# Hybrid decoder step: the dilated samples' window loads are requested in the paged stage's rings, and the next step's keys are turned ahead of the weights

## The reference, cut to what matters

```
DILATIONS = ((128, 1), (512, 4), (2048, 16))
def _dilated_sample(q, k_all, v_all, window, dil, n_buf):
    n_keys = window // dil
    idx = n_buf + jnp.arange(t)[:, None] - dil * jnp.arange(n_keys + 1)[None, :]
    kg, vg = k_all[:, idx], v_all[:, idx]
    sc = jnp.einsum('bqhd,bqjhd->bhqj', q, kg) / math.sqrt(HEAD_DIM)
    m = jnp.max(sc, axis=-1, keepdims=True)
    pw = jnp.exp(sc - m)
    l = jnp.sum(pw, axis=-1, keepdims=True)
    o = jnp.einsum('bhqj,bqjhd->bqhd', pw / l, vg)
    lse = (m + jnp.log(l))[..., 0]
```

## Time and profile before

| | us |
|---|---|
| time, median of 3 runs | 3216.09 (3215.17 to 3216.36) |
| profiled execution, its own time | 3219.56 |
| profiled execution, its span | 3218.0 |
| TensorE busy in the span | 2900.9 (90%) |
| VectorE busy | 1656.6 (51%) |
| ScalarE busy | 1463.8 (45%) |
| GpSimd busy | 632.9 (20%) |

### The profile page before, as it was taken

How to read it: one execution, slowest core, us unless ns; L and a number is a source line. 1 busy time by engine, 2 the same in 40 slices (tenths; PEclk the granted TensorE clock), 3 DMA queues, 4 the chain that set the end, 5 groups by cost and what they waited for, 6 DMA issues and landing times. The chain is left out here.

```text
span 3218.0 us, 46966 instructions
## 1 busy us (share of the span) xinstructions
PE 2900.9 (90%) x17542; PEld 2089.2 (65%) x17542; DVE 1656.6 (51%) x2702; ACT 1463.8 (45%) x2550; POOL 632.9 (20%) x908
## 2 busy tenths in 40 slices
PE   7999969999899999998999958888888873799998
PEld 5888848888555555555888845555555441588887
DVE  2000032222688888887666645555555434666663
ACT  3222131111577777776556525555555423333332
POOL 0000001111122222221033343443333200000000
PEclk9999989999899999998999979999999986899999
DMA  6656655554301010103223329999999886333321
GB/s 202 207 204 210 223 186 196 198 192 170 120 1 40 1 40 1 43 8 82 75 71 81 81 92 421 420 420 420 420 421 420 351 329 223 130 104 104 104 84 41
DMA packets 209508, 574.12 MB, mean 178 GB/s; under 512 B 39840, under 2 KB 108928, under 8 KB 173472
## 3 DMA queue, kind: packets, MB, share of 16 engines
q0 software_dynamic: 45568, 348.22, 27.5%
q1 hardware_dynamic: 163744, 223.27, 21.1%
HBM read 494.67 MB, written 143.73 MB: 198 GB/s over the span
## 5 line engine op out<-in xcount | busy, mean ns | idle before, releaser
L1512 DVE COPY sbs_kT<-sbs_ps_T 128x512 f32<-128x512 f32 x256 | 271.9, 1094 | 267.8 <-PE sbs_ps_T L1674 267.7
L465 PE MATMUL proj_ps_G<-proj_w_hi,proj_xT_hi 128*128 128x512 f32 x1024 | 399.8, 390 | 1.6 <-DVE proj_xT_lo L326 1.6
L469 PE MATMUL proj_ps_G<-proj_w_hi,proj_xT_lo 128*128 128x512 f32 x1024 | 398.6, 389 | 0.0
L467 PE MATMUL proj_ps_G<-proj_w_lo,proj_xT_hi 128*128 128x512 f32 x1024 | 398.5, 389 | 0.0
L404 ACT ACTIVATE proj_out<-proj_ps_G,proj_stat 128x512 f32<-128x512 f32 (+1 forms) x136 | 93.5, 689 | 581.2 <-PE proj_ps_G L469 574.2
L1674 PE MATMUL sbs_ps_T<-held,sbs_k_ring 128*128 128x128 f32 x2048 | 281.5, 293 | 41.5 <-ACT sbs_kT L1595 39.1
L1674 PEld LDWEIGHTS sbs_ps_T<-held,sbs_k_ring 128*128 128x128 f32 x2048 | 250.4, 153 | 84.4 <-ACT sbs_kT L1595 42.1
L674 POOL CAST sbp_sp_hi<-sbp_sp 128x512 fp32r<-128x512 f32 (+3 forms) x320 | 172.3, 553 | 505.3 <-DVE sbp_sp L716 495.2
L1595 ACT ACTIVATE sbs_kT<-sbs_ps_T 128x512 f32<-128x512 f32 x256 | 260.1, 1115 | 5.2 <-PE sbs_ps_T L1674 4.9
L716 DVE SCALAR_TENSOR_TENSOR sbp_sp<-sbp_Z,sbp_el 128x512 f32<-128x512 f32 (+3 forms) x320 | 180.0, 603 | 118.9 <-ACT sbp_el L794 118.5
L465 PEld LDWEIGHTS proj_ps_G<-proj_w_hi,proj_xT_hi 128*128 128x128 f32 x1024 | 192.2, 188 | 41.3 <-DVE proj_xT_lo L326 1.8
(11 more groups left out here) (289 smaller groups left out, 5803.6 us busy)
## 6 DMA issues: line engine op xcount, KB each, us to landing
out_k_win_s<-in_cache_k_win POOLq DMA_DIRECT2D x16, 2044.0 KB, 8.3
out_v_win_s<-in_cache_v_win POOLq DMA_DIRECT2D x16, 2044.0 KB, 8.3
proj_out<-in_w_in SPq DMA_DIRECT2D x32, 512.0 KB, 5.7
dls_k_in<-in_cache_k_win SPq DMA_DIRECT2D x16, 1024.0 KB, 10.9
dls_v_in<-in_cache_v_win SPq DMA_DIRECT2D x16, 1024.0 KB, 14.6
merge_o<-scratch_o_dil SPq DMA_DIRECT2D x48, 256.0 KB, 4.7
proj_x_in<-in_x_prompt SPq DMA_DIRECT2D x16, 512.0 KB, 4.3
scratch_xT_hi<-proj_xT_hi SPq DMA_DIRECT2D x16, 512.0 KB, 4.8
```

The source lines that it names most:

```text
L465: nc.tensor.matmul(ps_G[0:n, g, :], xT_hi[:, slot, k, 0:n], w_hi[:, k, cols], start=(k == 0), stop=False)
L467: nc.tensor.matmul(ps_G[0:n, g, :], xT_hi[:, slot, k, 0:n], w_lo[:, k, cols], start=False, stop=False)
L469: mm = nc.tensor.matmul(ps_G[0:n, g, :], xT_lo[:, slot, k, 0:n], w_hi[:, k, cols], start=False, stop=(k == KC - 1))
L1512: nc.vector.tensor_copy(by_lane(kT[:, j, :, :])[:, :, i, :], ps_T[:, x % TB, :].rearrange("p (a n) -> p a n", a=PAIRS)).then_inc(kT_odd, 1)
```

## The change

It has five parts.

- The rings `k_ring` and `v_ring` of the paged stage are allocated outside it and are used by the dilated samples too, in place of `k_in` and `v_in`. `kT` holds one chunk instead of two. The identity matrix and `own` are read from `held`, where the paged stage has them already.
- SP requests the new queries and keys of the dilated samples in the paged stage, behind the store of sample 6.
- Once the last page has landed (`v_loaded[7]` at its last count), SP requests the 8 chunks of keys and the 8 chunks of values of step 0, 16 MB, still in the paged stage. The store of the last sample's row comes behind these 16 loads in SP's list, and the wait for all stores behind that.
- In the dilated samples SP loads the mask, the counts and `pick16`, then the new values; for step 1 each key chunk is requested when the slot's tiles of step 0 have been turned, and the value chunks after `weigh(0)`.
- The keys of (1,0) are turned, copied and scored ahead of turning the weights of step 0, on TensorE, ACT and DVE.

One clearing of semaphores with its barrier moves from between the paged stage and the dilated samples to between these and `merge`.

```diff
+def window_new(held):
+    at = 8 * W - 2 * W - 248
+    return held[0:NS, at:at + 2 * W].rearrange("p (i c) -> p i c", c=W)
+
+def window_chunk(src, b, c):
+    rows = src[0].rearrange("b s h d -> b s (h d)")
+    if c == 0:
+        return rows[b, WIN - 512:WIN, :].rearrange("(n p) c -> p n c", p=P)
+    return rows[b].rearrange("(p r) c -> p r c", r=16)[:, 0:DEC_S, :]
...
@@ stick_breaking_sample, SyncE @@
-            for b in range(DEC_B):
+            def store(b):
                 sp.wait_ge(row_copied, b + 1)
                 sp.dma_start(t["o_sb_s"][b * DEC_S:(b + 1) * DEC_S, :], o_row[:, :]).then_inc(stored, 16)
+
+            for b in range(DEC_B - 1):
+                store(b)
+            w_new = window_new(held)
+            sp.dma_start(w_new[:, 0, :], t["q_dl_s"]).then_inc(win_new_loaded, 16)
+            sp.dma_start(w_new[:, 1, :], t["k_win_s"][0].rearrange("b s h d -> b s (h d)")[:, WIN - DEC_S:WIN, :]) \
+                .then_inc(win_new_loaded, 16)
+            sp.wait_ge(v_loaded[RING - 1], 16 * (NC * N // RING))
+            for x in range(RING):
+                sp.wait_ge(k_turned, GP * (NC * N - RING + x + 1))
+                sp.dma_start(k_ring[:, x, :, :], window_chunk(t["cache_k_win"], x % NC, x // NC)).then_inc(win_k_loaded[x], 16)
+            for x in range(RING):
+                if x % NC == 0:
+                    sp.wait_ge(av_done, N - 1 + x // NC)
+                sp.dma_start(v_ring[:, x, :, :], window_chunk(t["cache_v_win"], x % NC, x // NC)) \
+                    .then_inc(win_v_loaded[x // NC], 16)
+            store(DEC_B - 1)
             sp.wait_ge(stored, 16 * DEC_B)
...
@@ dilated_sample @@
-        ident = m.sb("ident", [P, P])
+        ident, own = (paged_constants(held)[n] for n in ("ident", "own"))
...
-        k_in = m.sb("k_in", [P, E, NA, W])
-        v_in = m.sb("v_in", [P, 2, E, NA, W])
-        v_new = m.sb("v_new", [DEC_S, E, W])
-        kT = m.sb("kT", [P, 2, E, PAIRS, 512])
+        kT = m.sb("kT", [P, E, PAIRS, 512])
...
@@ dilated_sample, SyncE @@
-            sp.dma_start(ident[:, :], t["ident"][:, :]).then_inc(new_loaded, 16)
-            sp.dma_start(qk_new[:, 0, :], t["q_dl_s"]).then_inc(new_loaded, 16)
-            sp.dma_start(qk_new[:, 1, :], k_new).then_inc(new_loaded, 16)
+            for buf, n in ((mask, "win_mask"), (count, "win_count"), (pick, "pick16")):
+                sp.dma_start(buf[:, :], t[n][:, :]).then_inc(consts, 16)
             for st in range(STEPS):
-                for c in range(2):
-                    for e in range(E):
-                        if st + c > 0:
-                            sp.wait_ge(turned, tile_of(st, c, e, 0) - (E - 1) * NA)
-                        sp.dma_start(k_in[:, e, :, :], chunk(k_c, E * st + e, c)).then_inc(k_loaded[e], 16)
-                    if st == 0 and c == 0:
-                        for buf, n in ((mask, "win_mask"), (count, "win_count"), (own, "own_head4"), (pick, "pick16")):
-                            sp.dma_start(buf[:, :], t[n][:, :]).then_inc(consts, 16)
                 if st > 0:
+                    for c in range(2):
+                        for e in range(E):
+                            sp.wait_ge(turned, tile_of(st - 1, c, e, NA - 1) + 1)
+                            sp.dma_start(k_ring[:, E * c + e, :, :], window_chunk(t["cache_k_win"], E * st + e, c)) \
+                                .then_inc(k_loaded[E * c + e], 16)
                     sp.wait_ge(av_done, st)
-                for c in range(2):
-                    for e in range(E):
-                        sp.dma_start(v_in[:, c, e, :, :], chunk(v_c, E * st + e, c)).then_inc(v_loaded[c], 16)
...
+                    for c in range(2):
+                        for e in range(E):
+                            sp.dma_start(v_ring[:, E * c + e, :, :], window_chunk(t["cache_v_win"], E * st + e, c)) \
+                                .then_inc(v_loaded[c], 16)
+                sp.dma_start(v_new[:, :, :], v_new_d[E * st:E * st + E].rearrange("b s c -> s b c")) \
+                    .then_inc(v_new_loaded, 16)
...
@@ dilated_sample, VectorE, in weights(st) behind the maximum @@
+                if st + 1 < STEPS:
+                    keys_to_sbuf(dve, nc.vector.tensor_copy, 1, st + 1, 0)
                 dve.wait_ge(exp_done, st + 1)
...
@@ dilated_sample, ScalarE @@
                 nc.scalar.activation(s[:, :], s[:, :], ACT.Exp, bias=stat[:, st, 0:1]).then_inc(exp_done, 1)
+                if st + 1 < STEPS:
+                    keys_to_sbuf(act, plain, 0, st + 1, 0)
...
@@ dilated_sample, TensorE @@
+            turn_keys(0, 0)
+            score(0, 0)
             for st in range(STEPS):
-                for c in range(2):
-                    turn_keys(st, c)
-                    score(st, c)
+                turn_keys(st, 1)
+                score(st, 1)
+                if st + 1 < STEPS:
+                    turn_keys(st + 1, 0)
+                    score(st + 1, 0)
                 turn_weights(st)
                 weigh(st)
...
@@ build @@
-            stick_breaking_sample(nc, t, held, paged_loaded)
-        nc.clear_and_free_semaphores([dil_qk_loaded, paged_loaded])
...
+            with nc.sbuf_tensor("sbs_k_ring", [P, 8, 4, W], F32) as k_ring, nc.sbuf_tensor("sbs_v_ring", [P, 8, 4, W], F32) as v_ring:
+                stick_breaking_sample(nc, t, held, paged_loaded, k_ring, v_ring, win_k_loaded, win_v_loaded, win_new_loaded)
+                dilated_sample(nc, t, held, k_ring, v_ring, win_k_loaded, win_v_loaded, win_new_loaded)
+        nc.clear_and_free_semaphores([dil_qk_loaded, paged_loaded, win_new_loaded] + win_k_loaded + win_v_loaded)
         nc.all_engine_barrier()
-        dilated_sample(nc, t)
         merge(nc, t)
```

More of the change, by code:

```diff
@@ L1328, in _, with stick_breaking_sample @@
                         turn_in(p + 1, f, OB[:, :])
-def stick_breaking_sample(nc, t, held, paged_loaded):
+def window_new(held):
[6 more added lines that the diff above has]
+    return rows[b].rearrange("(p r) c -> p r c", r=16)[:, 0:DEC_S, :]
+def stick_breaking_sample(nc, t, held, paged_loaded, k_ring, v_ring, win_k_loaded, win_v_loaded, win_new_loaded):
     C = H * DEC_S
@@ L1750, in _, with dilated_sample @@
             pick_rows(DEC_B - 1)
-def dilated_sample(nc, t):
+def dilated_sample(nc, t, held, k_ring, v_ring, k_loaded, v_loaded, new_loaded):
     C = H * DEC_S
@@ L1764, in dilated_sample @@
         m = Mem(nc, ctx, "dls")
-        ident = m.sb("ident", [P, P])
+        ident, own = (paged_constants(held)[n] for n in ("ident", "own"))
         mask = m.sb("mask", [P, KEYS])
         count = m.sb("count", [P, KEYS])
-        own = m.sb("own", [P, W])
         pick = m.sb("pick", [P, E * DEC_S])
-        qk_new = m.sb("qk_new", [NS, 2, W])
+        qk_new = window_new(held)
+        v_new = held[0:DEC_S, 2 * W - 384:6 * W - 384].rearrange("p (e c) -> p e c", c=W)
         q_pad = m.sb("q_pad", [P, DEC_B, PAIRS * (C + 8)])
@@ L1819, in dilated_sample @@
         TILES_PER_STEP = 2 * E * NA
[L1821 to L1827 removed]
+        v_new_d = t["v_win_s"][0].rearrange("b s h d -> b s (h d)")[:, WIN - DEC_S:WIN, :]
         block = ctx.enter_context(nc.Block())
@@ L1923, in plain @@
                 return nc.scalar.activation(out, src, ACT.Copy)
+            keys_to_sbuf(act, plain, 0, 0, 0)
             for st in range(STEPS):
-                for c in range(2):
-                    keys_to_sbuf(act, plain, 0, st, c)
+                keys_to_sbuf(act, plain, 0, st, 1)
                 act.wait_ge(max_done, st + 1)
                 nc.scalar.activation(s[:, :], s[:, :], ACT.Exp, bias=stat[:, st, 0:1]).then_inc(exp_done, 1)
+                if st + 1 < STEPS:
+                    keys_to_sbuf(act, plain, 0, st + 1, 0)
                 act.wait_ge(p_turned, st + 1)
@@ L1953, in turn_keys @@
                             pe.wait_ge(copied[(tt - 3) % 2], (tt - 3) // 2 + 1)
-                        if st > 0 and tt - TILES_PER_STEP * st < 3:
+                        if st > 0 and c == 1 and tt - tile_of(st, 1, 0, 0) < 3:
                             pe.wait_ge(p_copied[0], st)
@@ L1972, in score @@
                         mm = nc.tensor.matmul(Sc[e * C:(e + 1) * C, c, :], q_pad[:, E * st + e, pr * C:(pr + 1) * C],
-                                              kT[:, c, e, pr, :], start=(pr == 0), stop=(pr == PAIRS - 1))
+                                              kT[:, e, pr, :], start=(pr == 0), stop=(pr == PAIRS - 1))
                 if c == 1:
@@ L2004, in weigh @@
                         mm = nc.tensor.matmul(O[e * C:(e + 1) * C, :], pT[:, x, e * C:(e + 1) * C],
-                                              v_in[:, x // NA, e, x % NA, :], start=False, stop=(x == NT - 1))
+                                              v_ring[:, E * (x // NA) + e, x % NA, :], start=False, stop=(x == NT - 1))
                 mm.then_inc(av_done, 1)
@@ L2524, in build @@
             dilated_prompt(nc, t, held, dil_qk_loaded, paged_loaded)
```

(10 more changed lines are left out.)

33 lines of the change are left out of this document (10 added, 23 removed).

## The result

| | before | changed |
|---|---|---|
| median, us | 3215.17 (3207.44 to 3216.36, 5 runs) | 3232.51 (3229.27 to 3235.54, 5 runs) |
| profiled execution, its own time | 3219.56 | 3230.36 |
| its span | 3218.0 | 3228.5 |

The ratio is 1.0062, 95% interval 1.0049 to 1.0075: 15.8 to 24.1 us slower on 3215.17. The two medians are 17.3 us apart. The forecast was 3232.1, 16.0 us slower, from a median before of 3216.09.

A forecast was written before the change was run, and what follows sets the result against it. DMA bounds the paged stage's end, while the dilated samples are a chain with waits. A 29.3 us later start less 13.3 saved gives +16.0 on the median 3216.09: 3232.1 us, range 3222 to 3240.

The forecast's parts named there:

- The store behind the loads: End of paged stage: last store lands only with the 16 loads, so the dilated samples begin 29.3 us later.
- The rival that SP is only held in its issue: End of paged stage: store lands once SP's last load is accepted; +1.0 us in all, 3217.1; chance 0.05.
- Start of the stage: Dilated samples: first scores 12.0 us behind the start instead of 18.0, saving 6.0 us.
- Turn (0,1): Dilated samples: this turn of keys falls from 10.71 to 8.66 us, saving 2.05.
- The gap: Dilated samples: keys of (1,0) handled in the gap of the weights; 24.3 us become 22.4, saving 1.9.
- First weighing: Dilated samples, weigh(0): at full clock 8.2 us instead of 11.49, saving 3.3.
- Behind the weighing nothing changes: Dilated samples after weighing: no change in time; step 1's values just hidden, new values' row first on the queue.
- The sum: Whole kernel: 29.3 us later start less 13.3 us saved in the stage, +16.0 us.
- the rival on bandwidth: The 16 early loads run at 332 GB/s because chunks of 2 KB and 8 KB rows mix; +26, 3242 us; chance 0.04.

The follow-up runs named there:

- half the loads: Changed kernel with step 0's eight value loads moved to the dilated samples, last store on SP behind the eight key loads: ratio 0.9990, median 3211.49 us.
- another queue: Changed kernel with the last sample's store issued by ScalarE on its own queue: 1.0001; with only key loads in the paged stage as well: 0.9978.
- the late wait: Only key loads early, SP's loads reordered: last store moved from ScalarE to SP, its landing waited for at the dilated samples' end; 0.9937, median 3195.87 us.
- two runs: Changed kernel with the last store on ScalarE's queue (1.0001, median 3214.69 us), or on SP between key and value loads (1.0004, 3215.21 us).
- the two runs with the old order: Changed kernel with keys of (1,0) turned and scored behind weighing step 0 again: 1.0060, median 3235.32 us; on a slower chip 1.0035.
- the run with the new values first: Changed kernel with step 1's new values loaded ahead of its eight value loads: 1.0021 on a slower chip, beside 1.0034 for the changed kernel there.

## Why the prediction was right, step by step

- **The store behind the loads: right.** It was forecast to land with the last load, 44.8 us behind the first key load's issue; it was 44.2. The loads were to begin 14.1 us ahead of the copied row; 14.1. Behind the landing I had taken 1.9 us of barriers, with the clearing that moves; it was 1.16. So the start came 28.0 us later, not 29.3. The store landed 0.1 us behind the last load, and the experiments with half the loads, another queue and the late wait show that it is this wait. The forecast wanted the store issued after 2590; 2587.26 is 6.1 us early like everything in this trace.
- **The rival that SP is only held in its issue: wrong as the whole, right as a part.** SP's last load was accepted at 2587.21, 13.2 us behind the row. Had the store alone been mended, this limit would have stood in its place and taken all the gain, as two runs showed.
- **Start of the stage: saved 6.0 forecast, 6.3 measured** (scores 11.69 us behind the first DMA). **Turn (0,1):** 2.05 and 2.0 (2620.55 to 2629.25). **The gap:** 22.4 us and 22.54, saved 1.8. **First weighing:** 8.2 and 8.13, saved 3.4. In the changed kernel its 72 products took 1.06 and 7.07 us, and the two runs with the old order had 11.6 and 11.5 us for it again.
- **"Behind the weighing nothing changes": wrong, by 2.3 us.** I wrote that the new values' row comes first on the queue. In the new code it stands behind the eight value loads, where in the code before it stood between them. TensorE waited 2.69 us for it, 1.9 more than its 0.83 before (issued at 2667.38, it was there at 2684.2, 0.9 us ahead of the last value load); and the clearing that moves made the end 3.01 instead of 2.59 us. It is the same mechanism as the store's, and I had not applied it there; the run with the new values first had the 0.83 us again. The stage saved 11.2 us, not 13.3.
- **The sum:** +28.0 - 11.2 = +16.8 in the traces, +16.0 forecast. Two small errors went opposite ways, -1.3 us at the start and +2.1 in the stage, so the mechanism was right and the closeness of the sum is partly luck. So is the median, 0.4 us from the forecast: the median before had moved by 0.9, and the changed kernel's five runs spread over 6.3.
- **A misreading that cost nothing:** the rival on bandwidth gives the 2 KB rows to the keys and the 8 KB rows to the values. By `window_chunk` the chunks c = 0 have the short runs and c = 1 the long ones, in keys and values alike. The 16 loads ran at 399 GB/s in 2566:2604, near the 414 that I had taken.
- **The two rules.** The rule of the Trainium skill, "DMA: Bandwidth & Descriptors", "Rules for kernel authors", to issue early and wait late, is borne out by these runs: the stage took 92.61 to 98.55 us in every version with early loads, against 106.28, and moving the wait late took the start from 5.65 to 1.50 us behind the row. By the same page of the Trainium skill, "Queues, rings and completion order", completion is not in order for one issuing engine. Here that did not help a store of four rows: with key loads ahead it waited 10.0 us and landed 0.1 us behind the last of them.

## What to carry to other kernels

Before putting prefetches on a queue at the end of a stage, list what small transfer comes behind them and who waits for it: if it is on the same queue, that wait lasts until the whole prefetch has landed. Count also how long the issuing engine is held, because a barrier at the stage's end waits for its list and not only for its data. If the small transfer is not needed at once, move its wait, not the transfer; and order the loads of one queue by when each is needed, the small ones first.

## What the runs showed of the hardware

- SP is held by its own loads. Eight of 1 MB were issued in 6.5 us on an empty queue, the next eight took 20.7, and 12.5 when they began 8 us later. In both cases SP was free 27 us behind the first issue. The last load was issued at 2586.6 and landed 17.4 us later.
- A store of four rows behind 1 MB loads on the same queue landed 0.1 us behind the last of them, with 8 loads ahead (2586.43 against 2586.3) and with 16 (2604.13 against 2604.0).
- The same store on another queue, beside the loads, landed 4.0 us behind its issue and 4.8 us ahead of the last load, against 1.1 us behind its issue on idle engines.
- A wait in front of products at half clock (1.2 GHz, granted 0.50) was partly free in one pair of traces. TensorE came back to full clock (2.4 GHz) 4.6 us behind the start of the second weighing where it had waited, and 6.9 us behind it where it had not; so the run that waited 2.0 us longer lost only 0.8.
- One chip gathered pages at 344 instead of 420 GB/s and took 4.6% longer for the kernel before, while the 16 window loads took 44.9 us on it and 44.2 on the first.
